# A two-layer diffusion backbone on one core: a held expert tile regrouped as 64 tokens by two slots, its first loads issued a tile earlier, and the latents' Fourier mixing moved from one stage to the one before

## What is computed

```python
def _fnet(f):
    ff = f.reshape(bsz, L, FNET_GROUPS, FNET_GDIM)
    y = jnp.fft.fft2(ff, axes=(1, 3), norm="ortho").real
    return y.reshape(bsz, L, FNET_W)
...
        act = jax.nn.gelu(jnp.einsum("tkd,td->tk", u_tab[eb], hb))
        return jnp.einsum("tk,tkd->td", gb * act, v_tab[eb])
```

## Time and profile before

| | us |
|---|---|
| median of three runs | 4364.73 |
| lowest, highest | 4364.39, 4365.87 |
| the profiled execution | 4367.23 |
| its span, first to last instruction | 4365.4 |
| mean granted PE clock | 0.973 of full |
| busy: PE, DVE, ACT, POOL | 3693.1, 3006.0, 1720.2, 1645.7 |
| moved by DMA | 1506 MB, 345 GB/s on average |
| projection of the latents (stage 2 above) | 2310.8 to 2690.6 |
| branches beside the context (stage 3 above) | 2690.6 to 2765.5 |

### The profile page before, as it was taken

One profiled execution on the slowest core, in us unless ns is written; L12 is line 12 of the kernel. 1 busy time (PEld: TensorE's weight loads), 2 busy tenths in 40 slices (PEclk: granted clock), 3 DMA queues, 4 the chain that ended last, 5 costly groups with the idle time before them and its releaser, 6 DMA issues. The chain is left out here.

```text
span 4365.4 us, 55131 instructions
## 1 busy us (share of the span) xinstructions
PE 3693.1 (85%) x18945; PEld 1903.6 (44%) x18945; DVE 3006.0 (69%) x6251; ACT 1720.2 (39%) x5270; POOL 1645.7 (38%) x1508
## 2 busy tenths in 40 slices
PE   7998998988888887888886888888898888888777
PEld 3566854533433433433432335775443343343222
DVE  3964666975775875875875885557797687687444
ACT  2223623444344344344342454353444433433333
POOL 0004513443443443444443432352444444444332
PEclk9999999999999999999998999899999999999999
DMA  8360159999999999999999997015999999999997
GB/s 336 122 239 29 37 198 367 416 421 421 418 415 422 414 417 421 407 420 422 410 412 369 408 394 303 2 37 190 404 422 421 421 421 421 421 413 421 422 421 325
DMA packets 238985, 1506.07 MB, mean 345 GB/s; under 512 B 28433, under 2 KB 33617, under 8 KB 71153
## 3 DMA queue, kind: packets, MB, share of 16 engines
q0 software_dynamic: 184320, 1342.26, 74.7%
q1 hardware_dynamic: 54384, 160.28, 9.9%
HBM read 1490.32 MB, written 12.12 MB: 344 GB/s over the span
## 5 line engine op out<-in xcount | busy, mean ns | idle before, releaser
L2831 PE MATMUL ps<-low,pediag 128*128 128x512 f32 x2180 | 1058.7, 615 | 226.1 <-ACT pediag L2741 219.3
L2606 DVE CUSTOM_DVE_ANT_0 low<-low,hc 128x1024 f32<-128x1024 f32 x545 | 667.8, 1225 | 359.3 <-DMA low<-in_experts_dram,eid 342.0
L2585 POOL DMA_INDIRECT low<-in_experts_dram,eid x539 | 595.0, 1104 | 812.4 <-PE ps L2831 783.2
L2733 ACT ACTIVATE low<-peact 128x1 f32<-128x1 f32 x1152 | 232.1, 201 | 1335.0 <-DVE peact L2606 1334.0
L2831 PEld LDWEIGHTS ps<-low,pediag 128*128 128x128 f32 x2180 | 388.9, 192 | 824.5 <-ACT pediag L2741 499.4
L2741 ACT ACTIVATE pediag<-cst,low 128x128 f32<-128x128 f32 x1152 | 462.5, 402 | 42.1 <-PE ps L2831 4.5
L2831 PE MATMUL ps<-wide_a,pediag 128*128 128x512 f32 x640 | 307.8, 612 | 54.4 <-ACT pediag L2741 54.2
L2736 ACT ACTIVATE low<-low,gw 128x1 f32<-128x1 f32 x1152 | 339.1, 294 | 37.4
L2831 PE MATMUL ps<-wide_b,pediag 128*128 128x512 f32 x640 | 303.3, 605 | 50.7 <-ACT pediag L2741 48.5
L2060 PEld LDWEIGHTS ps<-qkvT,arena 128*128 128x128 f32 x2560 | 312.0, 193 | 75.4 <-issue 75.4
L2060 PE MATMUL ps<-qkvT,arena 128*128 128x128 f32 x2560 | 313.1, 276 | 2.4 <-ACT qkvT L2024 2.4
(11 more groups left out here) (497 smaller groups left out, 5773.9 us busy)
## 6 DMA issues: line engine op xcount, KB each, us to landing
pjdot<-in_mod_t_dram SPq DMA_DIRECT2D x64, 512.0 KB, 5.2
arena<-in_w_mod_dram SPq DMA_DIRECT2D x24, 1024.0 KB, 14.4
arena<-in_peer_wq_dram SPq DMA_DIRECT2D x8, 2048.0 KB, 17.1
low<-in_experts_dram,eid POOLq DMA_INDIRECT x609, 8.7
pjw<-in_w_cols_dram SPq DMA_DIRECT2D x18, 512.0 KB, 3.7
plw<-in_w_cols_dram SPq DMA_DIRECT2D x18, 512.0 KB, 8.1
x_rows<-low SPq DMA_DIRECT2D x10, 512.0 KB, 7.7
qkvT<-mod_rows SPq DMA_DIRECT2D x9, 512.0 KB, 7.6
```

Source lines behind the costliest of these rows:

```text
L2585: nc.gpsimd.indirect_dma_start(ring.row(g), None, table, bass.IndirectOffsetOnAxis(eid[:, j % 2, k:k + 1], 0)).then_inc(ring.landed(g), 16)
L2606: nc.vector.tensor_tensor_reduce(out=dot_out if final else ring.row(g)[:, 0:D], in0=ring.row(g)[:, 0:D], in1=hc[:, j % 2, :], scale=1.0, s ...
L2733: nc.scalar.activation(ge[:, g % 2, 0:1], act_v[:, j % 2, k:k + 1], ACT.Gelu_apprx_tanh).then_inc(gelu_ready, 1)
L2831: last = nc.tensor.matmul(ps[:, half, :], diag[:, g % DIAGS, :], ring.row(g)[:, D + half * 512:D + (half + 1) * 512], start=k == 0, stop=k ...
```

## The change

- **Slots.** A held step is now 64 tokens by two slots: partitions 0 to 63 hold slot s, partitions 64 to 127 slot 64 + s of the same 64 tokens. Steps 0 to 63 serve the first 64 tokens, 64 to 127 the others. The weights form a 128 by 64 matrix, which sums both slots in one product. All 128 steps are added on PE, as two matmuls of 512 columns with 64 output partitions each: the left half of v goes to PSUM partitions 0 to 63, the right half to 64 to 127 of the same bank. DVE's adds are gone, and all row buffers are freed by PE. There are four diagonal buffers instead of three.
- **Spreading.** Expert numbers, router weights and the 128 token rows are copied into the new arrangement by SBUF to SBUF DMAs: the numbers in the expert stage (four DMAs with 256 B pieces, POOL waits for them before the first held gather), the rows (two DMAs, then one) and the router weights (four) at the start of the projection stage. DVE's first dot waits for the rows, ACT's first weight for the router weights.
- **First loads.** `h_turned` (2 MB) is loaded in the expert stage once the last tile's queries are done, the first three weight chunks (1.5 MB) there after the expert numbers; all go to the arena. Chunks 3 to 5 are issued at the projection stage's start behind the spreads, later ones each after chunk c - 3.
- **Fourier.** The chunk order is 4 convolution, 2 Fourier, 12 of q, k, v. PE does the first Fourier products after chunks 6 to 9 (two each, before the sum of squares), ACT copies them after its chunks 7 to 10; the 512-point products follow on PE after chunks 11 to 14 (four matmuls each), and ACT's two copies after chunk 15. The tables are loaded behind chunk 6, the z weights after chunk 14. Silu and square come two chunks later than before (LAG 8 instead of 6), the last two silus between the z rows, and DVE's taps move with them. The branches stage has no Fourier work left except ACT's two copies into their place.
- **Branches stage.** The held result lies half in the wrong partitions; DVE copies these halves out, PE moves them with two matmuls by a piece of the identity, and DVE does four multiplications of 64 partitions instead of an add of two halves and one multiplication.

```diff
 class HeldTile:
...
+    def spread(self, sp, out, src, sem):
+        for half in range(2):
+            for part in range(2):
+                sp.dma_start(out[part * 64:(part + 1) * 64, half * 64:(half + 1) * 64],
+                             src[half * 64:(half + 1) * 64, part * 64:(part + 1) * 64]).then_inc(sem, 16)
+    def spread_rows(self, sp):
+        h = self.kit.hc
+        for part in range(2):
+            sp.dma_start(h[part * 64:(part + 1) * 64, 0, :], h[0:64, 1, :]).then_inc(self.rows_in, 16)
+        sp.wait_ge(self.rows_in, 32)
+        sp.dma_start(h[0:64, 1, :], h[64:128, 1, :]).then_inc(self.rows_in, 16)
...
             if g >= HELD_RING:
-                self.free(pool, g - HELD_RING)
+                pool.wait_ge(self.summed, g - HELD_RING + 1)
...
-            if g >= 2:
-                self.add(dve, g - 2)
...
+            if g == 0:
+                act.wait_ge(self.gw_in, 64)
             act.wait_ge(self.dotted, g + 1)
...
+            act.wait_ge(self.weighed, g + 1)
+            if g >= HELD_DIAGS:
+                act.wait_ge(self.summed, g - HELD_DIAGS + 1)
+            self.nc.scalar.activation(self.diag[:, g % HELD_DIAGS, :], self.kit.packed("I")[:, 0, :], ACT.Copy,
+                                      scale=self.coef[:, g:g + 1]).then_inc(self.diag_ready, 1)
...
+            pe.wait_ge(self.diag_ready, g + 1)
+            for half in range(2):
+                last = self.nc.tensor.matmul(self.kit.ps[half * 64:(half + 1) * 64, self.BANKS[g // 64], :],
+                                             self.diag[:, g % HELD_DIAGS, :],
+                                             self.rows[g % HELD_RING][:, D + half * 512:D + (half + 1) * 512],
+                                             start=g % 64 == 0, stop=g % 64 == 63)
+            last.then_inc(self.summed, 1)
```

In `projection_latents`, SP:

```diff
-                for t in range(NL):
-                    sp.dma_start(hT[:, :, t * P:(t + 1) * P], h_d[t].rearrange("p (k n) -> p k n", k=KD)
-                                 ).then_inc(h_in, 16)
+                held.spread_rows(sp)
+                held.spread(sp, held.gw, kit.gw[:, held.j % 2, :], held.gw_in)
+                sp.wait_ge(held.row_saved, 16)
                 for c, off in enumerate(chunks):
...
+                    if c == 2 * RING:
+                        for s in range(2):
+                            sp.dma_start(dft_l[:, :, s, :], kit.dft_l[s].rearrange("(t p) n -> p t n", p=P)
+                                         ).then_inc(dft_in, 16)
+                    if c == SEQ_AT + NL + 1:
+                        sp.wait_ge(seq_ready, NFN)
                         sp.dma_start(wz, kit.w_z[L].rearrange("p (k n) -> p k n", k=KD)).then_inc(wz_in, 16)
```

PE, after the eight matmuls of chunk c (HALF_AT is 6, SEQ_AT is 11):

```diff
+                    t = c - HALF_AT
+                    for i in range(2 if 0 <= t < NL else 0):
...
+                        nc.tensor.matmul(ps[:, 5 + i, 0:2 * P], fT[:, i, t * P:(t + 1) * P], kit.c2("C64"),
+                                         start=True, stop=True).then_inc(half_ready, 1)
+                    t = c - SEQ_AT
...
+                    for i in range(2 if 0 <= t < NL else 0):
+                        for s in range(2):
+                            last = nc.tensor.matmul(ps[:, 6 + i, :], half[t][:, i, s, :], dft_l[:, t, s, :],
+                                                    start=(t, s) == (0, 0), stop=(t, s) == (NL - 1, 1))
```

ACT, after the evacuation of chunk c and ahead of silu and square:

```diff
+                    t = c - HALF_AT - 1
+                    for i in range(2 if 0 <= t < NL else 0):
+                        act.wait_ge(half_ready, 2 * t + i + 1)
+                        nc.scalar.activation(half[t][:, i].rearrange("p s n -> p (s n)"), ps[:, 5 + i, 0:2 * P], ACT.Copy
+                                             ).then_inc(half_read, 1)
+                    if c == SEQ_AT + NL:
+                        for i in range(NFN):
+                            act.wait_ge(seq_ready, i + 1)
+                            nc.scalar.activation(fT[:, i, :], ps[:, 6 + i, :], ACT.Copy).then_inc(seq_read, 1)
```

In `branches_beside_context` PE's Fourier loop, `seq(0)` and `seq(1)` are removed, as are ACT's eight copies and the loads of the tables. PE has instead:

```diff
+                pe.wait_ge(far_read, 2)
+                for at, rows in ((lo, hi), (hi, lo)):
+                    last = nc.tensor.matmul(ps[at, 7, :], ident[:, rows], far[:], start=True, stop=True)
```

DVE:

```diff
+                nc.vector.tensor_copy(far[hi, :], ps[hi, 1, :]).then_inc(far_read, 1)
+                nc.vector.tensor_copy(far[lo, :], ps[lo, 3, :]).then_inc(far_read, 1)
...
+                for rows, cols, bank in ((lo, left, 1), (hi, right, 3), (lo, right, 7), (hi, left, 7)):
```

In `peer`, SP, behind its last wait:

```diff
+                if held:
+                    sp.wait_ge(sc.q_ready, HP * (N - 1) + LATE)
+                    for t in range(NT - NC):
+                        sp.dma_start(held.hT[:, :, t * P:(t + 1) * P], kit.h_d[t].rearrange("p (k n) -> p k n", k=KD)
+                                     ).then_inc(held.h_in, 16)
+                    sp.wait_ge(sc.eid_ready, late_numbers + N - 1)
+                    held.spread(sp, kit.eid2, eid[:, (N - 1) % 2, :], held.eid_in)
+                    for c in range(PL_RING):
+                        sp.dma_start(held.w[:, c], w_chunk(kit, L + 1, latent_chunks()[c])).then_inc(held.w_in, 16)
```

POOL, ahead of the first held gather:

```diff
-                    pool.wait_ge(sc.eid_ready, late_numbers + N - 1)
+                    pool.wait_ge(held.eid_in, 64)
```

More of the change, by code:

```diff
@@ L306, in __init__ @@
[L306 to L315, removed]
@@ L392, in pe @@
         for g in range(self.sums, self.sums + n):
[L393 to L398, removed]
-                                                 start=i == 0, stop=i == self.n_pe[SLOTS] - 1)
-                last.then_inc(self.summed, 1)
+            pe.wait_ge(self.diag_ready, g + 1)
[5 more added lines that the diff above has]
+            last.then_inc(self.summed, 1)
         self.sums += n
@@ L744, in projection_latents @@
         ZH = ZA // 2
-        two = lambda at: kit.arena[:, at:at + 2 * SEQ].rearrange("p (c n) -> p c n", c=2)
+        hT = held.hT
+        two = lambda i: room[:, i * 2 * SEQ:(i + 1) * 2 * SEQ].rearrange("p (c n) -> p c n", c=2)
         wz = kit.arena[:, 0:KD * ZA].rearrange("p (k n) -> p k n", k=KD)
-        at = KD * ZA
-        aT, gT, pT, yT = (two(at + i * 2 * SEQ) for i in range(4))
-        sq, root = aT, kit.arena[:, at + 2 * SEQ:at + 3 * SEQ]
+        aT, gT, pT, yT = (two(i) for i in range(4))
+        dft_l = kit.arena[:, 0:NL * 2 * SEQ].rearrange("p (t s n) -> p t s n", t=NL, s=2)
+        in_gates = room[:, 2 * SEQ:4 * SEQ]
+        behind = PL_FREE + 2 * D + 2 * ROWS * W
+        half = [part.rearrange("p (t c s n) -> p t c s n", t=2, c=2, s=2)[:, i]
+                for part in (in_gates, kit.arena[:, behind:behind + 8 * P]) for i in range(2)]
+        sq, root = aT, room[:, 2 * SEQ:3 * SEQ]
         at = PL_SPREAD
@@ L881, in _ @@
                 TAPS_EACH = -(-2 * CONV_K // NQKV)
-                for c in range(NF):
+                for c in range(NQKV + LAG):
                     n = c - LAG
@@ L925, in _ @@
                 held.all_landed(pool)
-PL_FT = KD * (GW + 4 * H) + 8 * SEQ
+PL_RING = 3
+PL_HT = KD * (GW + 4 * H)
+PL_FT = PL_HT + 8 * SEQ
 PL_SPREAD = PL_FT + 4 * SEQ
@@ L1029, in _ @@
             def _(pe):
-                def seq(c):
-                    for i in range(NL):
-                        for s in range(2):
-                            last = nc.tensor.matmul(ps[:, 6 + c, :], half[:, i, c, s, :], dft_l[:, i, s, :],
-                                                    start=(i, s) == (0, 0), stop=(i, s) == (NL - 1, 1))
-                    last.then_inc(seq_ready, 1)
                 def turn(t):
@@ L1099, in _ @@
                 link = linker(dve, dve_step)
-                for c in range(2):
-                    last = nc.vector.tensor_tensor(two(moved)[:, c, :], two(yacc)[:, c, :], ps[:, 1 + 2 * c, :], ALU.add)
-                link(last)
+                nc.vector.tensor_copy(far[hi, :], ps[hi, 1, :]).then_inc(far_read, 1)
+                nc.vector.tensor_copy(far[lo, :], ps[lo, 3, :]).then_inc(far_read, 1)
                 for c in range(2):
@@ L1168, in _ @@
                     nc.scalar.activation(csq[:, c, :], acc[:, c, :], ACT.Square).then_inc(csq_ready, 1)
-                for n in range(2 * NL):
-                    half_copy(n)
                 act.wait_ge(x_in, 16)
```

187 lines of the change are left out of this document (85 added, 102 removed).

## The result

The changed kernel takes 4392.6 us (median of 4 runs, 4387.9 to 4395.0) beside 4365.3 us before (4364.4 to 4372.3): ratio 1.0052, interval 1.0040 to 1.0065. The forecast was 4363 us, no change. The medians differ by 27.3 us, and the ratio, whose interval reaches that far, amounts to 23. The profiled execution's span is 4386.1 us, 20.7 over that of before: it is the fastest of its four, and the one before lies above its median. The table accounts for these 20.7 us.

What follows compares the result with a forecast made beforehand. Bounds: DMA in the expert stage and to chunk 8, a PE and ACT loop in chunks 9 to 17. Sum 0 - 4 + 11 + 1 + 3 - 11.5 = -0.5, 4364.2 at the median, 1 off: 4363 us, range 4345 to 4382.

Steps and rivals of the forecast that it cites:

- item 1: Projection start: seven loads move into the expert stage, stage begins at 2322.3; gain 0 (bounds -4 and +6).
- The early loads come too late: Rival, projection start: expert numbers' spread lands late, DMA engines run dry; +5 to +10, about 4373; chance 0.02.
- 3 us for the rows and 4.5 for the rest: Projection start: time for small spreading DMAs, so ACT starts 7.5 us in (bounds 4 and 14).
- Item 2: Seventh held gather to chunk 8: DMA-bound, chunk 8 at 2473 to 2475 instead of 2478.05; -4 us.
- Item 3: Chunks 9 to 17, PE and ACT loop: 166 us against 155, +11, and +1 for the z weights' loads.
- 1 us *off* for fewer such spells: Chunks 9 to 17 and z rows: fewer PE waits mean fewer 1.2 GHz spells; 1 us off the forecast.
- Item 4: z rows: about 13.6 us for three rows and 19 for the first, against 57.6 before; +3 us.
- Item 5: Branches stage: modulation rows 5 us earlier, no second Fourier half on PE; -11.5 us (bounds -8 and -13).
- the 67: Branches stage: a length above 67 us would show the forecast wrong; 63 to 64 instead of 75 was expected.
- The held step: PE: two column halves at once 0.86, column changes 0.29, weight load 0.05, together 1.20 us (bounds 1.15 and 2.06).
- The change of columns costs more: Rival, PE's held steps: at 1.5 us per step +22, 4385, chance 0.20; halves in turn about 4446, 0.03.
- The stalls take the Fourier work in: Rival: items 3 and 4 cost 3 us instead of 15, 4351; with the start's gain 4338; together chance 0.27.

Runs made afterwards that it cites:

- e1: Changed kernel with the whole block of early transfers (turned rows, expert numbers' spread, three weight chunks) ahead of the loop's last iteration; 4384.1 us, ratio 1.0033.
- e2: Changed kernel with only the spread of the expert numbers moved ahead of the loop's last iteration; 4384.2 us, ratio 1.0034.
- e5: e3 with the turned rows held tile by tile, each partition's 4 KB of a tile in one piece; 4377.0 us, ratio 1.0022.
- e4: e3 without the Fourier work in the projection stage (products, copies and tables); 4373.3 us, ratio 1.0007.
- e6: e5 with the Fourier tables' loads issued at chunk 10 instead of chunk 6; 4371.2 us, ratio 1.0009.
- e3: e1 with the router weights and token rows also spread ahead of the loop's last iteration; 4385.3 us, ratio 1.0039.
- e7: e6 with ACT's copies of the half transforms moved between the next chunk's third and fourth held slots; 4371.3 us, ratio 1.0006.
- e9: e7 with the three weight chunks issued right behind the turned rows; 4370.0 us, ratio 1.0000.
- e10: e9 with ACT's square root taken behind the first five held slots of the z rows; 4367.6 us, ratio 0.9998.
- e8: Changed kernel with only the turned rows' form altered to 4 KB pieces, loads left in their late place; 4391.5 us, ratio 1.0055.
- e11: e9 with both halves of a held slot's sum sent through the same 64 columns; 4453.8 us, one run.

## Why the prediction was wrong

**The step that failed is item 1**, "Seven loads (3.67 MB) move into the saturated expert stage", "the stage begins at 2322.3". The stage did begin at 2322.1, for another reason: the loads never moved, they followed the last tile's store, and the engines ran dry instead. The right number for the start was luck: it came from a wrong mechanism, and that mechanism hid that the spreads and the gathers would be late together. The seventh held gather went out at 2347.7 where I had 2332, and these 15.7 us are nearly all of the 16.9 by which the first two stretches missed. What I should have traced is the line above the block: SP's last loop iteration waits for the last tile's rows. I had listed this as a rival ("The early loads come too late"), with the spread's place behind `h_turned` in it, but at +5 to +10 and 0.02; it was +22.0 up to chunk 0 and +12.9 up to chunk 8. Within that step, "3 us for the rows and 4.5 for the rest" is the mis-sized term: 11.7 and 10.2 us, since both land among six gathers of 1.05 MB. I had thought of "an idle queue", and it was not idle. Up to chunk 0, e1 and e2 each gave back 8 us and e5 19 (102.2 to 83.1), and e5 shows what item 1 meant: there the last rows are stored 59.7 us behind the store of `h_turned`, 9.2 later than before, close to my 11.5.

**Item 2** was right in kind: share 1.01, 417 GB/s. From the seventh gather to chunk 8 it took 141.6 us, where I had 141 to 143; a stretch that begins 15.7 us later ends as much later. The tables' cost by e4 and e6 is 3.3 to 3.6 us in the interval of chunk 5 and 0.4 to 1.6 in the next, 4.0 to 4.9 together, where I had 5.2.

**Item 3** forecast 18.4 us for three intervals and 18.7 for four. The four are 18.69 to 18.70, to the second digit, with PE never waiting:

```profile
2568.52 1.08 PE L381 MATMUL ps<-low,parts 128*64 128x512 f32 x4
2569.53 3.70 PE L802 MATMUL ps<-arena,wide_a 128*128 128x512 f32 x8
2573.16 1.02 PE L812 MATMUL ps<-wide_a,arena 128*8 128x512 f32 x2
2574.11 1.12 PE L782 MATMUL ps<-arena,plw 128*128 128x512 f32 x2
```

The three (chunks 9 to 11) took 19.9, 19.9 and 20.9, 5.5 us more than 55. The timeline of PE behind chunk 10:

```profile
2530.86 1.13 PE L782 MATMUL ps<-arena,plw 128*128 128x512 f32 x2
2535.09 1.98 PE L381 MATMUL ps<-arena,parts 128*64 128x512 f32 x4 [3.10 <-ACT parts L372]
2536.99 3.78 PE L782 MATMUL ps<-arena,plw 128*128 128x512 f32 x4
2540.71 1.08 PE L381 MATMUL ps<-low,parts 128*64 128x512 f32 x4
```

PE waits 3.1 us for ScalarE's chain, and what follows runs at half the pace: 1.98 us for a held step's passes instead of 1.08, 3.78 for four full passes instead of 1.98. The granted clock from 2534.5 to 2540 is 0.50, its lower level of 1.2 GHz:

```profile
2534.50:2540.00 5.50, 4.91 (x8) 1.47 (x8) 3.66 (x8) 3.55 (x14) 1.80 (x1) 0.50 0.75 294
```

In e6, chunks 10 and 11 have no such spell, behind waits of 1.70 and 3.10 us, and take 18.21 and 18.24, near my 18.4. Behind chunk 10:

```profile
2515.74 1.08 PE L383 MATMUL ps<-arena,parts 128*64 128x512 f32 x4 [3.10 <-ACT parts L374]
```

So the term left out is a spell at the lower clock behind the wait: 1.7 us in the intervals of chunks 9 and 10, 2.7 in that of chunk 11. I had taken 1 us *off* for fewer such spells. Which waits bring one changes from run to run. A wait of 3.5 us in the interval of chunk 16 brought none in the changed kernel (18.66 us) and one in each of e1, e2, e3, e5, e6 and e7 (20.3 to 21.2 us). What decides, I leave open.

**Item 4**: +3.5 for +3. **Item 5**: -7.9 for -11.5. The modulation rows came 5.2 us earlier and the last row was done 19.4 us behind the z rows, both as forecast. The rest of the chain, to the chunk products, took 10.7 us for my 7.3, as the bound of -8 had it: PE had waited 10.65 us for the rows and worked at the lower clock (0.50 from 2737 to 2751); its 32 passes for the gate columns took 6.98 us and had taken 4.07. The stage's 68.2 us are also above the 67 that I had named as a sign of being wrong. The profile after, for PE:

```profile
2737.42 1.97 PE L1069 MATMUL ps<-cst,hc 128*128 128x128 f32 x8 [10.65 <-DVE hc L1144]
...
2743.74 6.98 PE L1090 MATMUL ps<-ciwab,cihT 128*128 128x16 f32 x32 [1.20 <-ACT cihT L1201]
2750.56 13.14 PE L1098 MATMUL ps<-cihT,arena 128*128 128x256 f32 x48
```

**The held step**, the price that I was least sure of, is right: 2.06 us less two passes (0.86) is 1.20. The Trainium skill, "TensorEngine Tiling (Array Packing)", section "Tiling Modes", has the change of mode drain the engine. The trace agrees with a cost: four passes of 0.43 us in two column groups would be 0.86, and the step is 0.34 over that, weight loads included. How much of this is a drain no run shows.

**The rivals.** "The change of columns costs more" fell with the step's 1.20. "The stalls take the Fourier work in" had items 3 and 4 at 3 us, and they came out at 19.7. e4 takes its side in part: of PE's 15 us of products, leaving them out gave back about 7 in the chunks. With the queue's order, the form of `h_turned`, the place of the tables and that of the copies all mended (e9), the change is worth nothing: 1.0000, interval 0.9991 to 1.0009. This is the "no change" of the forecast, but not by its sum. In the trace of e10 (0.9998) the stretches of the table differ from the kernel before by +2.2 and -11.8 up to chunk 8 (forecast -4 for both), +12.1, 0.0 and -7.6 us.

## What to carry to other kernels

A transfer is as early as the last wait ahead of it on its queue, not as the block of code in which it stands: read what the issuing engine waits for just above, and who waits for each transfer behind. Let small transfers on which another engine's first step hangs go out ahead of bulk ones, and price them as the queue will be at that moment. Bytes moved from an empty stage into one whose DMA share is 1.00 cost about what they save: the tables cost 4.0 to 4.9 us early in the stage and 3.2 later, where the share was 1.02 as well. Read the share of the very chunks in which they will land.

## What the runs showed of the hardware

- Issuing four DMAs of 0.5 MB from one queue took 4.6 us with idle engines (changed kernel) and 35.4 to 35.6 us under gathers at 400 GB/s (e1, e3), when they were cut in pieces of 512 bytes; in pieces of 4 KB, 3.4 us under the same load (e5) and 2.2 with idle engines (e8). The bytes were the same, so it is the pieces that hold the issuer under load.
- Two copies of 256 KB within the core's memory took 11.7 us beside six gathers (2322.1 to 2333.8 in the changed kernel), 8.7 in e2, 16.8 in e5 and 23.7 in e9, where weight chunks were ahead of them (2296.6 to 2320.3).
- In the changed kernel waits of PE of 1.96 and 3.10 us were followed by spells at a granted clock of 0.50 that cost 1.7 and 2.7 us; in e6 the same wait of 3.10 us was followed by none. So one such wait can cost nearly as much again behind it, in some executions.
- Two float32 matmuls of 512 columns with 64 output partitions each, to the two halves of one PSUM bank, run side by side: their passes start 0.01 us apart, and in turn (e11) 128 such pairs cost 84 us more.
